# Subtracting the low parts of four split weights on GpSimd instead of VectorE in a hybrid decoder layer

## What is computed

```python
h = rmsnorm(x, g_pre_mix[l]) * (1.0 + scale_m) + shift_m
proj = h @ w_in[l]
(gq, gk, gv, gg, ga_low, dq, dk, dv, iq, ik, iw, bg) = jnp.split(proj, offsets, axis=-1)
...
o_a = gla_chunked(q_a, k_a, v_a, la.reshape(B, S, GLA_HEADS, GLA_DK))
o_a = rmsnorm(o_a, g_gla_out[l]) * jax.nn.silu(gg.reshape(B, S, GLA_HEADS, GLA_DV))
y_gla = o_a.reshape(B, S, GLA_V) @ w_proj_gla[l]
...
o_b = dsa_attention(q_b, k_b, v_b, qi, ki, wi)
y_dsa = o_b.reshape(B, S, DSA_W) @ w_proj_dsa[l]
gates = jax.nn.sigmoid(bg.reshape(B, S, N_BRANCHES, D))
mix = gates[:, :, 0] * y_gla + gates[:, :, 1] * y_dsa
out = mix @ w_out[l]
x = x + gate_m * rmsnorm(out, g_post_mix[l])
...
y = hier_moe(h, w_router_g[l], b_router_g[l], w_router_e[l], b_router_e[l],
             w_e_gate[l], w_e_up[l], w_e_down[l])
x = x + gate_f * rmsnorm(y, g_post_ffn[l])
```

## Time and profile before

| what | us |
|---|---|
| median of 3 runs | 828.47 (826.12 to 830.65) |
| the profiled execution's own time | 827.6 |
| its span, first to last instruction | 825.7 |
| PE busy | 704.6 (85%) |
| DVE busy | 410.9 (50%) |
| ACT busy | 278.7 (34%) |
| POOL busy | 124.2 (15%) |
| mean granted clock of PE | 0.932 of full speed |

### The profile page before, as it was taken

How to read it: one execution, slowest core, us unless ns; L and a number is a source line. 1 busy time by engine, 2 the same in 40 slices (tenths; PEclk the granted TensorE clock), 3 DMA queues, 4 the chain that set the end, 5 groups by cost and what they waited for, 6 DMA issues and landing times.

```text
span 825.7 us, 9553 instructions
## 1 busy us (share of the span) xinstructions
PE 704.6 (85%) x3383; PEld 444.3 (54%) x3383; DVE 410.9 (50%) x872; ACT 278.7 (34%) x503; POOL 124.2 (15%) x149
## 2 busy tenths in 40 slices
PE   2899989899998899999998899989887877977940
PEld 1347647566776677777886788733332322322310
DVE  3387846888898867654322737734211211211117
ACT  5223215454446668532223132231211211211124
POOL 3074924220001021000000001010100011001000
PEclk9999969899998899999999999999989998999985
DMA  9989710311211020202355341489999999999735
GB/s 338 386 317 348 297 65 1 111 49 55 102 60 43 2 102 2 84 19 102 102 204 203 139 165 54 191 308 419 420 420 419 421 421 418 420 421 421 312 124 209
DMA packets 45564, 179.50 MB, mean 217 GB/s; under 512 B 9566, under 2 KB 9672, under 8 KB 30156
## 3 DMA queue, kind: packets, MB, share of 16 engines
q1 hardware_dynamic: 39428, 166.26, 51.2%
q0 software_dynamic: 4928, 8.42, 2.9%
q10 hardware_dynamic: 1160, 4.20, 1.3%
HBM read 174.66 MB, written 12.59 MB: 227 GB/s over the span
## 4 chain that ended last, share of the span: by engine, by line
PE 73%; DVE 12%; issue 8%; ACT 4%; DMA 3%; SPq 0%; ACTq 0%; DVEq 0%; POOLq 0%; PEldq 0%
PE psA L470 11%; PE psA L471 10%; PE psA L472 10%; PE psG L853 8%; PE psA L874 7%; PE psS L853 6%; PE psA L462 4%; PE psT L840 2%; DVE mk_mem L1705 1%; DVE arena_r L1653 1%; PE psO L601 1%; DVE m L1704 1%; PE psT L588 1%; DMA arena<-in_w_out_dram 1%; PE psA L522 1%
## 5 line engine op out<-in xcount | busy, mean ns | idle before, releaser
L470 PE MATMUL psA<-arena_r 128*128 128x512 f32 x320 | 132.0, 413 | 1.7 <-DVE arena_r L1653 1.1
L471 PE MATMUL psA<-arena_r 128*128 128x512 f32 x320 | 127.9, 400 | 0.0
L472 PE MATMUL psA<-arena_r 128*128 128x512 f32 x320 | 127.5, 399 | 0.0
L853 PE MATMUL psG<-arena,kv 128*64 128x512 f32 x224 | 69.0, 686 | 14.9 <-issue 14.7
L1653 DVE TENSOR_TENSOR arena_r<-arena,arena_r 128x1024 fp32r<-128x1024 f32 (+1 forms) x37 | 60.5, 1661 | 38.3 <-ACT arena_r L1214 37.7
L470 PEld LDWEIGHTS psA<-arena_r 128*128 128x128 f32 x320 | 62.2, 194 | 22.7 <-issue 10.4
L472 PEld LDWEIGHTS psA<-arena_r 128*128 128x128 f32 x320 | 62.1, 194 | 13.8
L471 PEld LDWEIGHTS psA<-arena_r 128*128 128x128 f32 x320 | 62.3, 195 | 12.4 <-issue 0.2
L853 PE MATMUL psS<-arena,kv 128*64 128x512 f32 x208 | 60.0, 612 | 8.6 <-issue 8.6
L1214 ACT CAST arena_r<-arena 128x1024 fp32r<-128x1024 f32 (+1 forms) x31 | 49.9, 1630 | 21.5 <-DMA arena<-in_w_in_dram 10.7
L2102 DVE TENSOR_TENSOR sig_mem<-sig_mem,psG 128x256 f32<-128x256 f32 x8 | 4.9, 614 | 94.0 <-ACT sig_mem L1513 94.0
(11 more groups left out here) (393 smaller groups left out, 1282.0 us busy)
## 6 DMA issues: line engine op xcount, KB each, us to landing
arena<-in_w_e_gate_dram SPq DMA_DIRECT2D x27, 1024.0 KB, 25.1
arena<-in_w_e_up_dram SPq DMA_DIRECT2D x27, 1024.0 KB, 27.4
arena<-in_w_in_dram SPq DMA_DIRECT2D x11, 2048.0 KB, 8.4
arena<-in_w_e_down_dram SPq DMA_DIRECT2D x12, 1024.0 KB, 19.0
qs_mem<-in_w_e_down_dram SPq DMA_DIRECT2D x10, 1024.0 KB, 20.7
arena<-in_w_ada_dram SPq DMA_DIRECT2D x4, 2048.0 KB, 16.9
qT<-in_w_ada_dram SPq DMA_DIRECT2D x6, 1024.0 KB, 5.7
gvs<-in_w_ada_dram SPq DMA_DIRECT2D x5, 1024.0 KB, 6.5
```

The lines of the kernel that those rows point to most:

```text
L470: nc.tensor.matmul(acc, lhs[0], rhs[0], start=start, stop=False)
L471: nc.tensor.matmul(acc, lhs[0], rhs[1], start=False, stop=False)
L472: return nc.tensor.matmul(acc, lhs[1], rhs[0], start=False, stop=stop)
L853: last = nc.tensor.matmul(ps[g][64 * q:64 * q + 64, :].rearrange("p (g f) -> p g f", g=2), h2g[:, b, k, 64 * q:64 * q + 64], gu, start=(k ...
```

## The change

The 16 quarter subtractions of `in_units` leave DVE's stream and enter POOL's, as the same subtraction of 128 x 1024 numbers. They count a semaphore of their own, `lo_pool`, which PE waits for in place of `lo_ready`; the positions in `lo_ready` are renumbered (`lo_at`). POOL's stream is written out by hand: the subtractions stand between the exponents and the gains, and the exponents of chunk 0 come behind all four quarters of unit 0. A counter `idx_seen` is dropped and its increments go to `pstep`.

```diff
-        hi_units, lo_units = ((0,), (1, 2), (3,), ()), ((), (0,), (1, 2), (3,))
+        hi_units = ((0,), (1, 2), (3,), ())
+        lo_at = {key: 4 * n for n, key in enumerate(key for key in split_at if key not in in_units)}
...
             def split_wait(key, pieces=4):
                 pe.wait_ge(hi_ready, split_at[key] + pieces)
-                pe.wait_ge(lo_ready, split_at[key] + pieces)
+                if key in in_units:
+                    pe.wait_ge(lo_pool, 4 * in_units.index(key) + pieces)
+                else:
+                    pe.wait_ge(lo_ready, lo_at[key] + pieces)
...
-            for tt in range(TT):
-                gla_exponents(tt)
+            def split_lo(unit, *pieces):
+
+                key = in_units[unit]
+                src, lo, hi = splits[key]
+                for q in pieces:
+                    pool.wait_ge(hi_ready, split_at[key] + q + 1)
+                    part = slice(1024 * q, 1024 * (q + 1))
+                    pool.tensor_tensor(lo[:, part], src[:, part], hi[:, part], ALU.subtract).then_inc(lo_pool, 1)
+
+            def gate_gain(tt):
                 pool.wait_ge(gs_in, tt + 1)
...
+            split_lo(0, 0, 1, 2, 3)
+            gla_exponents(0)
+            split_lo(1, 0, 1, 2, 3)
+            gate_gain(0)
+            split_lo(2, 0)
+            gla_exponents(1)
+            gate_gain(1)
+            split_lo(2, 1, 2)
+            gate_gain(2)
+            split_lo(2, 3)
+            gla_exponents(2)
+            gate_gain(3)
+            split_lo(3, 0)
+            gla_exponents(3)
+            split_lo(3, 1, 2, 3)
...
-                pool.sem_inc(idx_seen, 1)
+                pool.sem_inc(pstep, 1)
...
-            act.wait_ge(lo_ready, split_at["h"] + 4)
+            act.wait_ge(lo_ready, lo_at["h"] + 4)
...
-                for q in lo_units[u % 4] if u < NU else ():
-                    split_lo(in_units[u // 4], q)
```

More of the change, by code:

```diff
@@ L345, in layer @@
         sin_in2, c32_ready, lnv_ready, lnq_ready, pstep_const = (sem(n) for n in ("sin_in2", "c32_ready", "lnv_ready", "lnq_ready", "pstep_const"))
-        fsq_in, idx_seen, ex_sub = sem("fsq_in"), sem("idx_seen"), sem("ex_sub")
+        fsq_in, ex_sub = sem("fsq_in"), sem("ex_sub")
+        lo_pool = sem("lo_pool")
         hi_ready, lo_ready = sem("hi_ready"), sem("lo_ready")
@@ L1100, in gla_exponents @@
                                        ALU.subtract).then_inc(ex_sub, 1)
+            def split_lo(unit, *pieces):
[6 more added lines that the diff above has]
+            def gate_gain(tt):
+                pool.wait_ge(gs_in, tt + 1)
+                g3 = gs[:, tt, :].rearrange("p (h n) -> p h n", h=GLA_H)
+                pool.tensor_tensor(g3, g3, g_out_b.unsqueeze(1).broadcast_to([P, GLA_H, P]), ALU.mult).then_inc(gs_ready, 1)
             pool.wait_ge(b_ready, 2 * TT)
@@ L1105, in _ @@
             pool.wait_ge(rowb_ready, 1)
-            for tt in range(TT):
-                gla_exponents(tt)
-                pool.wait_ge(gs_in, tt + 1)
-                g3 = gs[:, tt, :].rearrange("p (h n) -> p h n", h=GLA_H)
-                pool.tensor_tensor(g3, g3, g_out_b.unsqueeze(1).broadcast_to([P, GLA_H, P]), ALU.mult).then_inc(gs_ready, 1)
+            split_lo(0, 0, 1, 2, 3)
[13 more added lines that the diff above has]
+            split_lo(3, 1, 2, 3)
             pool.wait_ge(oa_ready, TT)
```

## The result

Before 827.79 us (median of 8 runs, 826.12 to 830.65), after 833.75 (8 runs, 832.32 to 839.23). The ratio is 1.0081, 95% interval 1.0060 to 1.0102: about 6 us slower. The forecast was 829.8 with a range of 819.5 to 837. The time lies inside that range, but on the side to which I had given 0.25; the slower rival's 834.5 is the number it came near. Counted as a change, the forecast's sum was +1.3 us, on the 828.47 of the first three runs, and the measured change is +6.0: the width of the range holds it, the sum does not.

A forecast was written before the change was run, and what follows sets the result against it. PE was taken to bound the attention loop, DVE close behind, POOL with room. Terms of -0.5 and +1.75 summed to +1.25 on 827.6, giving 828.9; against the median of 828.47 the forecast was 829.8, range 819.5 to 837.

The forecast's parts named there:

- slower rival: Pair 5: POOL's quarter 1 beats DVE's scaling to the ports, delaying PE there and in pair 6; +6, 834.5 us; chance 0.27.
- The bound: Attention loop: PE sets the pace, busy 159.3 of 170 us, DVE close behind; POOL, busy 14.9, has room.
- the two long waits: PE's waits of 2.0 us (pair 9) and 1.9 us (pair 11), low clock behind each; an earlier DVE is worth something.
- faster rival: POOL misses DVE's critical stretch in pair 10, relief shortens PE's waits, clock may stay high; -7.5, 821.0 us; chance 0.22.
- Price of a subtraction: Each moved subtraction costs DVE 1.22 us and was taken as 2.4 us on POOL, sixteen making 38 us.
- (1): Chunk 0's exponents move behind unit 0 and no longer stretch DVE's two L1728 before PE's first loop wait; gain 0.5 us.
- (2): Pairs 1 to 4: one or both scalings of pairs 1 and 2 slip about 2.3 us, as removed subtractions had cost; zero.
- (3): Pair 6: quarter 3 on POOL delays a scaling from 233.05 to 235.3; two removed subtractions, 2.3 us, pay; zero.
- (4): Pairs 7 and 8: DVE arrives earlier but chunk 0's gain holds the ports; zero, the 2.0 us wait stays.
- (5): Pair 10: products 1.8 us late, a scaling 2.25 later, minus 2.3 from removed subtractions; PE's turn loses 1.75 us.
- (6): Pairs 11 to 15: delays of chunk 3's clamp (1.6 us) and a pair 14 scaling (2.3) are covered or repaid; zero.

The follow-up runs named there:

- e8_ports_alone: Against before: all 16 subtractions stay on DVE; POOL, in its new order, adds twelve idle ones into unused memory; 846.8 us, ratio 1.0226.
- sixth experiment: The kernel before with one more POOL wait, so chunk 0's exponents start behind ACT's fourth quarter of unit 0; 826.58 us, ratio 0.9987.
- e2_fenced: The changed kernel with POOL waits holding quarters and the gains of chunks 0 and 2 behind DVE instructions they would stop; 826.18 us, ratio 0.9992.
- fifth experiment: Against before: no subtraction moved, only POOL's new order, gains of chunks 2 and 3 ahead of their chunks' exponents; 832.92 us, ratio 1.0058.
- e3: The changed kernel's POOL order, but only unit 1 subtracted on POOL, the other units on DVE; 833.43 us, ratio to before 1.0050 to 1.0092.
- e4: The changed kernel's POOL order, but only unit 2 subtracted on POOL, the other units on DVE; 834.1 us, ratio to before 1.0063 to 1.0105.
- e12: The changed kernel with chunk 2's gain and unit 2's later quarters held until pair 10's scalings are done; 830.23 us, ratio 1.0008.

## Where the prediction was right and where wrong, step by step

**The number** was right by luck. The range holds 833.75 only because the slower rival's number was taken in, and that rival laid its +6 on pairs 5 and 6; those are worth 2.0 us in the trace. Most of the loss stands in pair 10 and in the clock behind it.

**The bound** held in kind: PE sets the pace, and what DVE delays, PE waits for. That DVE's earliness at the two long waits was worth something was too hopeful in size: without any subtraction the median gains 1.6 us, not told from nothing, with the faster rival's number at -7.5.

**Price of a subtraction:** 2.4 taken, 2386 ns measured. The estimate worked out from the Trainium skill's GPSIMD Engine Reference (section 3.1) was 2.25; the measurement decides, and the difference of 0.14 us is small beside stops of 2 us.

**(1), exponents of chunk 0, -0.5:** held. In the profiles the first two pairs take 17.1 us where the exponents are late and the grant over 192 to 200 us is 0.79 (five kernels beside e8_ports_alone), and 17.6 where they are not late. The sixth experiment gives -1.4 by medians, with an interval that touches no change.

**(2), pairs 1 to 4, zero:** held; 2 to 5 takes 20.5 to 20.7 us in all but e8_ports_alone, though a scaling of pair 1 and one of pair 2 were stopped, to 2.22 us each. Of the 2.1 us that the first pairs won in the after profile, 0.5 are the exponents' and the rest is the clock's, as in e2_fenced.

**(3) and the slower rival's place, pairs 5 and 6:** this step failed. I let DVE win the race for the ports in pair 5. POOL's three quarters ran without a gap from 221.24, the second from 221.24 + 7.23 / 3 = 223.65, and the scaling came at 223.79: the tenth by which the rival had POOL ahead. Both scalings of pair 5 were stopped, 2.47 and 2.25, and one of pair 6, 2.44. In the profiles it is no toss either: 5 to 8 takes 24.2 us in all five kernels with unit 1 on POOL and nothing to hold it back. Its size was +2.0 us in the trace (5 to 8: 24.2 against 22.2), where the rival had 1.6 + 1.0 for PE.

**(4), pairs 7 and 8, zero:** held as far as the waits go; the 2.0 us wait of pair 9 stayed (L647, 2.0).

**(5), pair 10, +1.75:** the stops came as walked. The products began at 274.70 instead of 273.35, 1.35 late where I had 1.8, and the scaling was stopped 2.32 - 0.42 = 1.9 us where I had 2.25. PE's two waits grew from 1.9 to 1.3 + 2.2 = 3.5, that is by 1.6, against 1.75 forecast; it was spread over two waits, where I had expected one of 3 to 4. What failed is the term behind it: I priced the low clock that stands behind PE's wait at nothing in the sum and left it to the range. Pairs 10 to 12 took 3.8 us more, of which 1.6 is waiting; the other 2.2 I put down to the clock, whose grant fell from 0.84 to 0.73 over 270 to 302 us. The L1806 that was stopped, a copy of two elements per partition, I had not listed; I had the products themselves as the victim.

**(6), pairs 11 to 15, zero:** nearly. In the trace of after L1798 and L1799 are stopped by quarters 1 and 2, an L1889 by quarter 3. 12 to 15 takes 35.5 or 35.6 us in all five kernels with unit 3 on POOL and nothing to hold it back, and 35.0 or 35.1 in the others: 0.5 us that I had at zero.

**What the sum left out altogether** is the gains' own move. I walked the gain of chunk 2 in pair 10 only as the reason for which quarter 3 comes late. Alone it costs 5 us (fifth experiment), the same as both together. The parts aren't additive: order alone +5.0, unit 1 with it +5.9, unit 2 with it +6.6, all +6.0. A sum over pairs can't give this.

What doesn't add is the clock. Every timed run has its span and mean granted clock on record; span x (1 - clock) is at most what the clock took from it, since low clock may also fall where PE waits. As an estimate, the means over the runs against those of before on the same chip (the changed kernel against the mean of all four chips), good to about 1 us each:

| kernel | span | of it clock | rest |
|---|---|---|---|
| order alone (e5) | +4.0 | +3.5 | +0.5 |
| unit 1 and order (e3) | +5.4 | +2.5 | +2.8 |
| unit 2 and order (e4) | +6.1 | +4.3 | +1.8 |
| the change | +6.2 | +3.2 | +3.0 |
| the change, pair 10 clear (e12) | +0.2 | -2.1 | +2.2 |

The rests behave nearly as a sum: 0.5 for the order, 2.3 more for unit 1, 1.3 more for unit 2, and their 4.1 is not far from the 3.0 of the whole change; unit 1's 2.3 is also near the 2.0 of its stops in the trace. The clock's part is 2.5 to 4.3 us with every one of these disturbances, small or large, and absent with pair 10 clear, which still carries its rest of 2.2 and is level with before only by its higher clock. That a small stop in pair 10 brings it about as well as a large one is how I read this; the estimate's error leaves room for differences of 1 us.

What stays open is what sets that stretch off. The fenced kernel had it in its profile (0.50 over 276 to 284 us) without a stop in pair 10, and was fast all the same, since its other pairs were short; the profile of the kernel with pair 10 clear did not have it. Perhaps its presence is a matter of how often, and a stop makes it likelier or longer; that reading was not tested by profiles of several runs of one kernel.

## What to carry to other kernels

Before work goes from VectorE to GpSimd, list the VectorE instructions with SBUF on both sides that will run beside it, small ones of two elements per partition too, and count each moved GpSimd instruction as a stop of up to its whole length for the first of them; waits that hold GpSimd back until those are done cost nothing here, where GpSimd has slack, and took the loss from 6 us to none. Reordering GpSimd's other small instructions counts as a change of its own. Where stretches of low clock stand behind PE's waits, as here, don't only add up the stops: test the parts, since one of them may give nearly the whole.

## What the runs showed of the hardware

- An instruction's size does not protect it: L1806 with 128x2 elements took 2.06 us instead of 0.17, L1798 with 128x2 1.83 instead of 0.17, both beside a GpSimd subtraction. RECIPROCAL and TENSOR_SCALAR on 128x1 did not change (160 and 159 ns, 154 and 154), nor did MAX8 on SBUF (690 and 689 ns); in the profile of after some of each began while a subtraction ran on GpSimd.
- GpSimd's subtraction of 128x1024 takes 2386 ns with two full sources and 2380 with two broadcast ones; the multiplication L1114 of before, also of two broadcast inputs, takes 1897 ns. So broadcast operands by themselves are not what made that one short.
- One run's profile misleads in both directions: e12_pair10_clear's loop was 3.3 us shorter than before's in its profile, and yet it has no gain in its median, and e5_order took only 1.9 us more for the loop in its own while its median is 5 higher.
- TensorE's granted clock differs from run to run of the same kernel, and with it the time: 0.941 to 0.944 with 823.5 to 824.9 us against 0.930 to 0.933 with 829.0 to 832.9. That the difference lies in the stretch behind pair 10 is inferred from one profile.
